# Experts as one stream: rows and results through HBM scratch, and the next up projection inside the last down projection

## The reference

```python
def swiglu(h, w1, w3, w2):
    return (jax.nn.silu(h @ w1) * (h @ w3)) @ w2

def moe_swiglu(h, w_router, w1, w3, w2):
    logits = (h @ w_router).astype(jnp.float32)
    top_v, top_i = lax.top_k(logits, TOP_K)
    wts = jax.nn.softmax(top_v, axis=-1)
    combine = jnp.sum(jax.nn.one_hot(top_i, N_EXPERTS, dtype=jnp.float32) * wts[..., None], axis=-2)
    out = jnp.zeros_like(h)
    for e in range(N_EXPERTS):
        out = out + combine[..., e:e + 1] * swiglu(h, w1[e], w3[e], w2[e])
    return out
```

## Time and profile before

| | |
|---|---|
| median of 3 runs | 1764.06 us (1763.98 to 1764.47) |
| the profiled execution | 1764.39 us, its span 1762.7 us |
| PE busy | 1708.0 us, 97% |
| DVE busy | 1320.3 us, 75% |
| ACT busy | 1087.8 us, 62% |
| chain of waits | PE 91%, DVE 4%, issue 2%, ACT 2% |
| HBM read, written | 469.33 MB, 1.05 MB |

### The profile page before, as it was taken

One profiled execution on the slowest core, in us unless ns is written; L12 is line 12 of the kernel. 1 busy time (PEld: TensorE's weight loads), 2 busy tenths in 40 slices (PEclk: granted clock), 3 DMA queues, 4 the chain that ended last, 5 costly groups with the idle time before them and its releaser, 6 DMA issues.

```text
span 1762.7 us, 25440 instructions
## 1 busy us (share of the span) xinstructions
PE 1708.0 (97%) x9610; PEld 1484.8 (84%) x9610; DVE 1320.3 (75%) x1331; ACT 1087.8 (62%) x1039; POOL 7.1 (0%) x37
## 2 busy tenths in 40 slices
PE   7999999999999999899999999999999999999996
PEld 6989999999898999788788788788788788887885
DVE  6555566555655566688888898888888888988887
ACT  5535444343453544477777777777777777777775
POOL 1000000000000000000000000000000000000000
PEclk9999999999999999999999999999999999999999
DMA  8633448553563334599899899899899899998993
GB/s 275 187 120 120 130 156 289 189 178 99 195 193 120 120 122 160 187 368 379 303 372 383 293 372 375 308 368 375 300 380 379 296 367 343 332 377 315 367 376 127
DMA packets 237636, 471.35 MB, mean 267 GB/s; under 512 B 7590, under 2 KB 73712, under 8 KB 237568
## 3 DMA queue, kind: packets, MB, share of 16 engines
q1 hardware_dynamic: 235664, 468.22, 75.0%
q10 hardware_dynamic: 1648, 2.10, 0.3%
q0 software_dynamic: 256, 0.08, 0.0%
HBM read 469.33 MB, written 1.05 MB: 267 GB/s over the span
## 4 chain that ended last, share of the span: by engine, by line
PE 91%; DVE 4%; issue 2%; ACT 2%; DVEq 0%; DMA 0%; ACTq 0%; SPq 0%
PE bank L586 82%; PE bank L576 3%; PE bank L952 1%; DVE wlo L1748 1%; PE bank L919 1%; DVE x_sb L1792 1%; PE bank L810 1%; PE bank L781 1%; ACT yT_hi L1283 1%; PE bank L624 1%; DVE wlo L1390 0%; PE bank L763 0%; PE bank L636 0%; DVE yT_lo L1756 0%; ACT hT_hi L1331 0%
## 5 line engine op out<-in xcount | busy, mean ns | idle before, releaser
L1748 DVE TENSOR_TENSOR wlo<-raw,whi 128x2048 fp32r<-128x2048 f32 x336 | 766.8, 2288 | 103.9 <-ACT whi L1300 103.3
L1300 ACT ACTIVATE whi<-raw 128x2048 fp32r<-128x2048 f32 x336 | 643.5, 1918 | 207.1 <-PE bank L586 207.0
L586 PE MATMUL bank<-whi,yT_hi 128*128 128x512 f32 x1428 | 563.7, 395 | 12.3 <-DVE yT_lo L1756 8.6
L586 PE MATMUL bank<-whi,yT_lo 128*128 128x512 f32 x1428 | 557.1, 390 | 0.0
L586 PE MATMUL bank<-wlo,yT_hi 128*128 128x512 f32 x1428 | 556.5, 390 | 0.0
L1390 DVE TENSOR_TENSOR wlo<-raw,whi 128x2048 fp32r<-128x2048 f32 (+3 forms) x107 | 235.7, 2205 | 191.6 <-ACT whi L1088 191.3
L586 PEld LDWEIGHTS bank<-whi,yT_hi 128*128 128x128 f32 x1428 | 268.1, 188 | 72.7 <-DVE wlo L1748 16.1
L586 PEld LDWEIGHTS bank<-whi,yT_lo 128*128 128x128 f32 x1428 | 268.0, 188 | 57.2
L586 PEld LDWEIGHTS bank<-wlo,yT_hi 128*128 128x128 f32 x1428 | 268.3, 188 | 52.5
L1088 ACT ACTIVATE whi<-raw 128x2048 fp32r<-128x2048 f32 (+3 forms) x107 | 197.6, 1848 | 127.3 <-PE bank L586 113.8
L586 PE MATMUL bank<-hT_hi,whi 128*128 128x256 f32 x848 | 243.7, 287 | 3.1 <-DVE hT_lo L1412 1.8
(11 more groups left out here) (237 smaller groups left out, 1587.9 us busy)
## 6 DMA issues: line engine op xcount, KB each, us to landing
raw<-in_moe_w SPq DMA_DIRECT2D x338, 1024.0 KB, 7.1
raw<-in_w_in SPq DMA_DIRECT2D x36, 1024.0 KB, 5.3
raw<-in_dense_w SPq DMA_DIRECT2D x30, 1024.0 KB, 5.4
raw<-in_w_br SPq DMA_DIRECT2D x12, 1024.0 KB, 5.0
raw<-in_w_mkv SPq DMA_DIRECT2D x8, 1024.0 KB, 6.3
raw<-in_w_out SPq DMA_DIRECT2D x8, 1024.0 KB, 5.1
raw<-in_w_in SPq DMA_DIRECT2D x4, 768.0 KB, 7.2
raw<-in_w_uq SPq DMA_DIRECT2D x4, 576.0 KB, 5.2
```

The costliest lines, as they stand in the source:

```text
L586: ins = nc.tensor.matmul(bank, lhs(a, k), rhs(b, k), start=(start and k == chunks[0] and a + b == 0), stop=(stop and k == chunks[-1] and a ...
L1300: nc.scalar.activation(whi[:, (E0 + i) % SPLIT, :], raw[:, i % RAW, :], ACT.Copy).then_inc(hi_ready, 1)
L1748: V.tensor_tensor(wlo[:, s, :], raw[:, i % RAW, :], whi[:, s, :].bitcast(F32), ALU.subtract).then_inc(lo_ready, 1)
```

## The change

The experts are no longer separate passes of one loop body. Their program has the phases `head` (up projections of block 0, expert 0), `loop` (7 times: blocks 1 to 6 of one expert, block 0 of the next, the last down projection), `last` (blocks 1 to 6 of expert 7 and its combination) and `over` (the second pass, which doesn't run).

Rows: DVE makes the normalised rows times the gain (`rows_out`), and GpSimd writes each to its place in HBM scratch (`rows_by_slot`), twice, by indirect DMAs. ACT's queue loads the next expert's 128 rows in block 1 of the loop. PE transposes them (`rows_T`, 8 transposes) before the last w3 projection of block 6; ACT and DVE split them. Only expert 0 is still gathered by matmuls.

Results: in the loop ACT copies `ey` to SBUF and stores it to scratch (`y_by_slot`). During the last expert GpSimd fetches for each token its two results, and DVE adds them. The last expert is still scattered by matmuls.

Scratch is filled with zeros where no row may fall: 24 transfers of 0.5 MB behind weight loads of the first dense layer. The gain row is loaded by SP ahead of the last out projection's weights. In an up projection the four matmuls with the low part of a weight piece now come after the eight with the high part, with a wait of their own. `EARLY` is 4, and with the 4 pieces of `head` 8 pieces are planned ahead of the loop.

The core of the diff:

```diff
@@ -43,7 +43,7 @@
 RAW = 7
 MIX_RAW = 3
 SPLIT = 3
-EARLY = 2
+EARLY = 4
 MEM_AT = 6
...
+        def half_pieces(*blocks):
+            return [(kind, b, half) for kind, b in blocks for half in range(2)]
+
+        head_items = half_pieces(("w1", 0), ("w3", 0))
+        mid_items = [i for b in range(1, NM) for i in half_pieces(("w1", b), ("w3", b), ("w2", b - 1))]
+        items = {"head": head_items, "loop": mid_items + head_items + half_pieces(("w2", NM - 1)),
+                 "last": mid_items + half_pieces(("w2", NM - 1)),
+                 "over": head_items + mid_items + half_pieces(("w2", NM - 1))}
+        PER_E = len(items["loop"])
...
+        for n in range(HEAD + EARLY):
+            key = items["head"][n] if n < HEAD else items["loop"][n - HEAD]
+            piece(("e", DEPTH - 1, n), RAW, e_source(*key, 0))
...
-                pe.wait_ge(sel_ready, j + 2)
-                gather(("gather", 0), 0, j)
-                hidden_T(NM - 1)
-                gather(("gather", 1), 1, j)
-                down(NM - 1)
-
-                read(pe, ("selT", 0), j)
...
+            def up(phase, kind, b_, j, rows=None):
+
+                name = {"w1": "e1", "w3": "e3"}[kind]
+                b = claim((phase, name, b_), j)
+                for half in range(2):
+                    i = at[phase][kind, b_, half]
+                    w = e_high(phase, i, j)
+                    if rows is not None:
+                        rows(half)
+                    for k in range(4):
+                        for a in range(2):
+                            nc.tensor.matmul(b[:, :], hselT[a][:, half, tok(k)], w[:, k, :],
+                                             start=(half + k + a == 0), stop=False)
+                    w = e_low(phase, i, j)
+                    for k in range(4):
+                        ins = nc.tensor.matmul(b[:, :], hselT[0][:, half, tok(k)], w[:, k, :],
+                                               start=False, stop=(half == 1 and k == 3))
+                    e_mark(ins, phase, i, *([(name, b_)] if half else []))
...
+            def blocks(phase, j):
+
+                for b_ in range(1, NM):
+                    up(phase, "w1", b_, j)
+                    hidden_T(phase, b_ - 1, j)
+                    if phase == "loop" and b_ == NM - 1:
+
+                        pe.wait_ge(slots_moved, 32 * j + 16)
+                        rows_T(phase, j)
+                    up(phase, "w3", b_, j)
+                    down(phase, b_ - 1, j)
...
-            with pe.Fori(0, NE) as j:
-                job(j)
-            recording = False
+            with pe.Fori(0, NE - 1) as j:
+                blocks("loop", j)
+                up("loop", "w1", 0, j, lambda half: read(pe, ("loop", "rows", half), j))
+                hidden_T("loop", NM - 1, j)
+                up("loop", "w3", 0, j)
+                down("loop", NM - 1, j)
...
+            blocks("last", 0)
+            combine("last", 0)
...
+            empties = [rows_by_slot[i] for i in range(1, JOBS)] + [y_by_slot[i] for i in range(NE - 1, JOBS)]
+            assert len(empties) == N_ZEROED
+            to_zero = {}
+            for i, empty in enumerate(empties):
+                to_zero.setdefault((("w1", "w3")[i % 2], 0, 2 + i // 2 % (ND - 2)), []).append(empty)
...
+                if key == ("out", DEPTH - 1, 0, 0):
+                    reached(sp, ("ms", DEPTH - 1, XH - 1))
+                    sp.dma_start(gain_row, g_ffn[DEPTH - 1].partition_broadcast(P)).then_inc(gain_row_in, 16)
...
+                for empty in to_zero.pop(key, []):
+                    sp.wait_ge(zeros_made, 1)
+                    sp.dma_start(empty.rearrange("s (r c) -> s r c", c=SEQ),
+                                 zeros[:, :].unsqueeze(1).broadcast_to([P, D // SEQ, SEQ])).then_inc(zeroed, 16)
...
+            pool.wait_ge(slots_known, 1)
+            pool.wait_ge(zeroed, 16 * N_ZEROED)
+            pool.wait_ge(rows_scaled, T)
+            for t in range(T):
+                for n in range(2):
+                    nc.gpsimd.indirect_dma_start(
+                        out=rows_by_slot.rearrange("j s d -> (j s) d"),
+                        out_offset=bass.IndirectOffsetOnAxis(ap=slot_i[:, n, t:t + 1], axis=0),
+                        in_=rows_out[:, t, :], in_offset=None).then_inc(dispatched, 16)
+
+            pool.wait_ge(dispatched, 16 * 2 * T)
+            pool.wait_ge(hn_lo, T)
+            pool.wait_ge(slots_moved, 32 * (NE - 1))
+            for t in range(T):
+                for n in range(2):
+                    nc.gpsimd.indirect_dma_start(
+                        out=picked[t][:, n, :], out_offset=None, in_=y_by_slot.rearrange("j s d -> (j s) d"),
+                        in_offset=bass.IndirectOffsetOnAxis(ap=slot_i[:, n, t:t + 1], axis=0)).then_inc(picked_in, 16)
...
+                for b_ in range(1, NM):
+                    e_hi(phase, e_room(phase, "e1", b_), j)
+                    e_silu(phase, b_, j)
+                    if phase == "loop" and b_ == 1:
+
+                        act.wait_ge(dispatched, 16 * 2 * T)
+                        reached(act, (phase, "rows", 1), j - 1)
+                        act.dma_start(row_in_slot, rows_by_slot[1:][j]).then_inc(slots_moved, 16)
+                    e_hi(phase, e_room(phase, "eT", b_ - 1), j)
+                    hidden_hi(phase, b_ - 1, j)
...
+            with act.Fori(0, NE - 1) as j:
+                n_done = EARLY
+                blocks("loop", j)
+
+                e_hi("loop", e_room("loop", "e3", NM - 1), j)
+                reached(act, ("loop", "e3", NM - 1), j)
+                rows_hi_part("loop", j)
+                e_hi("loop", e_room("loop", "e1", 0), j)
+                e_silu("loop", 0, j)
+                e_hi("loop", e_room("loop", "eT", NM - 1), j)
+                hidden_hi("loop", NM - 1, j)
+                e_hi("loop", e_room("loop", "ey", 0), j)
+
+                act.wait_ge(slots_moved, 32 * j + 16)
+                for n in range(2):
+                    b = full(act, ("loop", "ey", n), j)
+                    free(nc.scalar.activation(y_slot[:, n * HALF:(n + 1) * HALF], b[:, :], ACT.Copy), ("loop", "ey", n))
+                for n in range(2):
+                    read(act, ("loop", "ey", n), j)
+                act.dma_start(y_by_slot[j], y_slot).then_inc(slots_moved, 16)
+                e_hi("loop", PER_E + EARLY, j)
...
+            dve.wait_ge(gain_row_in, 16)
+            for t in range(T):
+                V.scalar_tensor_tensor(out=rows_out[:, t, :], in0=x_sb[:, t, :], scalar=rin[:, 6 + t:7 + t],
+                                       in1=gain_row, op0=ALU.mult, op1=ALU.mult).then_inc(rows_scaled, 1)
...
+            def add_picked(t, n):
+
+                dve.wait_ge(picked_in, 16 * 2 * T)
+                if n:
+                    dve.wait_ge(x_summed, t + 1)
+                V.scalar_tensor_tensor(out=x_sb[:, t, :], in0=picked[t][:, n, :], scalar=gap[:, 3 - n, t:t + 1],
+                                       in1=x_sb[:, t, :], op0=ALU.mult, op1=ALU.add).then_inc(x_summed, 1)
```

616 lines of the change are left out of this document (358 added, 258 removed).

## The result

The changed kernel took 1710.55 us (median of 4 runs, 1710.04 to 1712.28) against 1764.02 us for the kernel before (4 runs, 1762.04 to 1764.47): ratio 0.9701, 95% interval [0.9684, 0.9718]. The forecast was 1709 us. The profiled execution of the changed kernel has a span of 1710.5 us, against 1762.7 us.

A forecast was written before the change was run, and what follows sets the result against it. PE's own work and the expert boundary, not the DMA, bound the expert stage. Gains 50.9 + 0.5 - 0.2 + 2.7 + 1.6 = 55.5 us off 1764.39 gave 1709 us, range 1702 to 1733.

The forecast's parts named there:

- The period: Expert loop: 118.9 us a period instead of 126.17, bounds 0 and 1.5 on the ACT order's 0.3; seven periods gain 50.9 us.
- Overlap: Expert boundary: next up projection directly before the last down projection covers ACT's and DVE's answer; boundary cost 8.5 us per expert.
- Rival D: Loop's edge: a wait on ACT's or DVE's order brings back 4 us a period, 1737 us; chance 0.11.
- High-first: Up projections: waiting for the low part only after eight matmuls (1.8 us) lets the row copies (1.2 us of ACT) pass.
- DMA: Expert loop: 45.1 MB in 118.9 us, 379 GB/s, fits with a 3% margin; no loss, bounds 0 and 12 us.
- Rival A: Expert loop: DMA holds only 374 GB/s with writes, 120.6 us a period, 1721 us; chance 0.13.
- rival C: Scratch traffic among the loads breaks streaming, from 357 GB/s downward; slower than before, 1781 to 1816 us; chance 0.04.
- Dispatch: Start of expert stage: POOL sends 4 x 0.5 MB to scratch at no cost, bounds 0 and 8 us.
- rival B: First dispatch is late and stops ACT by 5 to 10 us, once; 1717 us; chance 0.10.
- Start: Start of expert stage: DVE's longer chain loses 0.2 us, bounds 0 and 1.5; a removed split wait gains 0.5.
- 2.3 us: 2.7 gained: Before the last down projection: transposes, ACT, DVE and one DVE split make 2.3 us instead of 5.0.
- squares: 1.6 gained, bounds 0.8 and 2.2: Program's end: the 2.28 us prefetch split is gone, ACT's squares then end the chain; 1.6 us gained.

The follow-up runs named there:

- e8: Changed kernel without the row loads and result stores of the seven middle experts; 1710.0 us.
- e1: Changed kernel with the overlap undone: next expert's first up projection again behind this expert's last down projection; 1761.55 us, ratio 0.9983 to the kernel before.
- e2: Changed kernel with up projections taking a weight's low part in turn with the high part, as before the change; 1719.17 us.
- e3: Changed kernel with two more stores of 0.5 MB per expert period into spare scratch; 1710.1 us.
- e4: Changed kernel with six more stores of 0.5 MB per expert period into spare scratch; 1721.27 us.
- e11: The changed kernel once more, unedited, in the session of e12; 1710.71 us.
- e12: Changed kernel, last expert: picked-row additions a block earlier, last difference ahead of the last split, overflow flag read ahead of the combine; 1708.62 us.
- e10: e1 with 32 idle products put into PE's gap ahead of the loop's last down projection; 1761.11 us.
- e6: Changed kernel, last expert: picked-row additions one block earlier, last hidden tile's difference ahead of the last weight split on DVE; 1708.69 us.
- e9: e1 with the last hidden tile's copy one split earlier on ACT and its difference two splits earlier on DVE; 1723.3 us.

## Why the prediction was right

**The period (right, to 0.2 us).** Sum of PE's work 118.6, order on ACT 0.3, together 118.9; measured 119.08. e8 splits the excess: 118.81 without the two issues, so 0.27 for them, and 0.2 for what else the sum lacked. The mean period of before is (1747.33 - 863.58) / 7 = 126.25 by the same event as in the earlier trace rows, so seven periods gave 50.2 us where 50.9 were forecast.

**Overlap (right, but its weight was not seen).** The prediction took the whole boundary of 8.5 us off and put back 0.9 for the row transposes, without a price for the removal alone. e1 gives it: 3 us in all. PE is busy for 124.22 of 126.2 us in one expert of before (863.6 to 989.8 us) and for 118.86 of 119.0 us now, so of the 7.2 us gained 5.4 are work and 1.8 are waits. Without the overlap the work is gone as well, but PE waits 4.9 us a period, and 6 to 10 products behind that run at the lower clock. Before the change half of the gather of the next expert's rows (16 matmuls, 1.8 us) had stood in that wait, and 1.1 us of it were left. Rival D had the right mechanism and priced it at 4 us a period; e1 shows 7.

**High-first (right in effect, wrong in place).** The prediction said that without it the row copies would show. They do, by 0.5 us a period in e2; about as much of its worth again (4.2 us once, against 3.2 in six periods) lies behind the loop, where DVE's selection and additions would show.

**DMA (right).** 379 GB/s were forecast and measured. Rival A (374 GB/s) and rival C (under 357) fall with e3, which moves 388 GB/s at no cost. The Trainium skill, page Perfetto Trace Analysis, section Roofline, says that 358 GB/s is a core's share when both cores of a pair stream, and that a lone core can go to about 120% of it. The trace agrees in direction: e4 stops at 399 GB/s, 111%.

**Dispatch (right, rival B falls).** Four indirect writes take 0.95 to 1.06 us of POOL each, 1.26 to 1.36 us apart, against the 0.92 taken from a plain DMA, and are issued by 741 us; ACT never waits for them. Zeros: nothing that shows, as said. The prediction also weighed that POOL's issues could be held up by VectorE. The dispatch doesn't test it (DVE is busy 1.1 of the 4 us from 736 to 740), but the four indirect loads of the last expert do. POOL, then DVE at the same place:

```profile
1595.77 2.47 POOL L1200 DMA_INDIRECT hn<-y_by_slot,slot_i  x1 [0.31 <-issue]
1598.54 0.94 POOL L1200 DMA_INDIRECT pbuf<-y_by_slot,slot_i  x1 [0.30 <-issue]
```

```profile
1595.11 2.28 DVE L1924 TENSOR_TENSOR wlo<-raw,whi 128x2048 fp32r<-128x2048 f32 x1
```

The two issues that meet a weight split on DVE take 2.61 and 2.47 us and end 0.87 and 0.85 us after the split does; the two beside DVE's small operations take 0.94. The traces of e11 and e12 show the same, 0.84 to 0.86 us after the split's end. It costs nothing here, since nobody waits for them yet.

**Start (small miss).** Forecast 0.2 lost and 0.5 gained. The 0.2 had no ground in its own sum: 4.8 us of new work fit into 5.1 us of idle time. The first matmul is not later by more than the traces differ, and the first expert's transposes come 16.46 us behind it instead of 17.48: 1.0 gained, since the selection transposes left the first block along with the wait.

**The end (wrong size, twice).** The step "2.3 us: 2.7 gained" counted one DVE split ahead of the difference; there were an addition and two splits, and the gain was 1.8 us (to the down projection 3.22 us against 5.01). The step "squares: 1.6 gained, bounds 0.8 and 2.2" gave 0.5, under its lower bound. ACT's reading of the flag had stood there before the change too (first line below); the split that was removed had cost only the second wait:

```profile
1750.89 0.63 ACT L1101 ACTIVATE pbuf<-x_sb 128x512 f32<-128x512 f32 x1 [2.97 <-issue]
...
1752.20 0.63 ACT L1101 ACTIVATE pbuf<-x_sb 128x512 f32<-128x512 f32 x1 [0.59 <-DVE x_sb L1792]
```

Together the end gave 2.3 us where 4.3 were forecast. Not thought of at all was that the clock can fall in the new gap. In the profiled execution it did: 24 products take 7.4 us and not 5.73, and 1.65 of the 2.3 us are lost again.

**Sum.** 50.2 + 1.1 (start) + 0.2 (small parts ahead of the last transposes) + 1.8 - 1.65 + 0.5 = 52.2 = 1762.7 - 1710.5. Without the fallen clock it is 53.8, and the medians differ by 53.5. Forecast 55.5: of the error of about 2 us the end is 2.0 and the periods 0.7, and the start gave 0.8 back.

## What to carry to other kernels

When work is taken off the bounding engine, look at what it had been covering: the removal alone gave 3 us here, and the same removal with other work of the same stream put into the hole gave 53. Size a wait by everything that stands in the answering engine's queue, not by the shortest chain; moving two splits behind one small difference, and one behind the copy ahead of it, was worth 38 us in the serial loop. Where a gap on TensorE grows, allow for what the clock may take behind it. And before a microsecond in one trace is put down to a cause, or an edit is credited with removing it, trace the unedited kernel a second time: here that alone made 1.5 us go away.

## What the runs showed of the hardware

- A gap of 4.9 us on TensorE was followed by 6 to 10 products at the lower clock level each time (seven of seven in e1; granted clock 0.57 over four microseconds, products 0.43 us apart). Filled with idle products it was not (seven of seven in e10). A gap of 2.41 us was in four of nine traces, the same kernel falling in one trace and not in the other (0.62 over four microseconds in the one, 1.00 in the other). Gaps of 1.26 us (e6, e12) and 1.60 us (seven in e9) were not. The gap's length alone doesn't decide it: at the start of the expert stage gaps of 0.78 and 0.89 us were followed by a granted clock of 0.57 in e6 and e2 (737 to 741 us), and the same 0.78 us in the changed kernel was not.
- One core, loading weights and storing scratch together, moved 399 GB/s over 700 us when 405 were asked for; at 388 nothing is felt. The engines' share of busy time reads 1.02 to 1.04 in all three, so it does not tell how near the ceiling is; the landing time does (7.4 us at 379, 8.1 at 388, 14.7 at 399).
- Issuing an indirect load of 0.5 MB costs POOL 0.94 us, and 1.35 to 2.6 us where a weight split on DVE is under way; it then ends 0.84 to 0.87 us after the split (six issues in three traces).
- Reading a flag into a register and branching on it left ACT idle 3.0 us at the end, before the change and after. With the reading moved ahead and the branch left where it was (e12), the wait was 2.1 us and for data, so it was the reading.
